# Gated DeltaNet and sliding-window block on one core: GpSimd's weight splits moved behind the first softmax quotient, one sum moved from VectorE to ScalarE

## What is computed

```python
def hybrid_layer(x, norm_w, w_in, conv_w, a_log, dt_bias, gdn_norm_w, attn_sinks,
                 w_o_a, w_o_b, w_out, pos_bias):
    h = rms_norm(x, norm_w)
    z = h @ w_in
    (qa, ka, va, b_a, a_a, za, qb, kb, vb, zb, gate_a, gate_b) = jnp.split(z, SPLIT_POINTS, axis=-1)
    qkv = jax.nn.silu(causal_depthwise_conv(jnp.concatenate([qa, ka, va], axis=-1), conv_w))
...
    qa = l2_normalize(qa.reshape(B, T, GDN_HEADS, GDN_DK))
    ka = l2_normalize(ka.reshape(B, T, GDN_HEADS, GDN_DK))
...
    oa = gated_delta_rule(qa, ka, va, g, beta)
    oa = rms_norm(oa, gdn_norm_w) * jax.nn.silu(za.reshape(B, T, GDN_HEADS, GDN_DV))
    ya = oa.reshape(B, T, GDN_V_W) @ w_o_a
    ob = swa_sink_attention(...)
    ob = ob.reshape(B, T, SWA_Q_W) * jax.nn.silu(zb)
    yb = ob @ w_o_b
    merged = jax.nn.sigmoid(gate_a) * ya + jax.nn.sigmoid(gate_b) * yb
    return x + merged @ w_out
```

## Time and profile before

| | us |
|---|---|
| median of 3 runs | 2635.09 (2634.76 to 2636.34) |
| the profiled execution, its own time | 2636.74 |
| its span in the trace | 2634.9 |
| PE busy | 2594.6 (98%) |
| DVE busy | 1340.2 (51%) |
| ACT busy | 894.6 (34%) |
| POOL busy | 404.8 (15%) |
| SP waits for splits, 60 to 480 us | 355.6 in 48 waits |

### The profile page before, as it was taken

How to read it: one execution, slowest core, us unless ns; L and a number is a source line. 1 busy time by engine, 2 the same in 40 slices (tenths; PEclk the granted TensorE clock), 3 DMA queues, 4 the chain that set the end, 5 groups by cost and what they waited for, 6 DMA issues and landing times.

```text
span 2634.9 us, 50095 instructions
## 1 busy us (share of the span) xinstructions
PE 2594.6 (98%) x20276; PEld 2129.6 (81%) x20276; DVE 1340.2 (51%) x3401; ACT 894.6 (34%) x2886; POOL 404.8 (15%) x238
## 2 busy tenths in 40 slices
PE   7999999999999999999999999999999999999998
PEld 5777777888888888888888888888888888888887
DVE  6577777323266666612325666651223666665022
ACT  4454445332234344321114344432112333434001
POOL 3443334343210011000001011000000011010000
PEclk9999999999999999999999999999999999999999
DMA  7555455687653333355553433335546433333554
GB/s 246 191 205 199 164 185 198 244 282 288 239 182 129 131 135 135 135 192 209 183 215 142 141 131 137 130 125 208 208 176 230 141 119 135 130 131 129 204 211 175
DMA packets 96085, 467.06 MB, mean 177 GB/s; under 512 B 13808, under 2 KB 34544, under 8 KB 48880
## 3 DMA queue, kind: packets, MB, share of 16 engines
q1 hardware_dynamic: 65664, 427.85, 45.1%
q10 hardware_dynamic: 30192, 36.02, 4.6%
HBM read 361.00 MB, written 102.83 MB: 176 GB/s over the span
## 4 chain that ended last, share of the span: by engine, by line
PE 90%; DVE 5%; DMA 1%; POOL 1%; ACT 1%; issue 1%; ACTq 0%; SPq 0%; POOLq 0%; DVEq 0%
PE bank L1321 24%; PE bank L1323 22%; PE bank L1322 22%; PE last_banks L1444 3%; PE last_banks L1432 2%; PE bank L1510 1%; PE bank L1495 1%; PE bank L1424 1%; PE bank L1487 1%; PE bank L1555 1%; PE last_banks L1564 1%; PE bank L1545 1%; PE bank L1540 1%; PE last_banks L1561 1%; PE bank L1502 1%; DMA w_raw<-in_w_tiles 1%
## 5 line engine op out<-in xcount | busy, mean ns | idle before, releaser
L1321 PE MATMUL bank<-hT_hi,w_sl 128*128 128x512 f32 x2112 | 889.6, 421 | 0.0
L1323 PE MATMUL bank<-hT_hi,w_sl 128*128 128x512 f32 x2112 | 826.9, 392 | 0.0
L1322 PE MATMUL bank<-hT_lo,w_sl 128*128 128x512 f32 x2112 | 825.6, 391 | 0.0
L1323 PEld LDWEIGHTS bank<-hT_hi,w_sl 128*128 128x128 f32 x2112 | 396.4, 188 | 86.9
L1321 PEld LDWEIGHTS bank<-hT_hi,w_sl 128*128 128x128 f32 x2112 | 397.6, 188 | 76.7 <-issue 0.9
L1322 PEld LDWEIGHTS bank<-hT_lo,w_sl 128*128 128x128 f32 x2112 | 398.6, 189 | 58.9 <-issue 0.7
L441 POOL TENSOR_TENSOR w_sl<-w_raw,w_sl 128x1024 fp32r<-128x1024 f32 x90 | 218.2, 2428 | 344.4 <-ACT w_sl L525 335.1
L1001 DVE SCALAR_TENSOR_TENSOR area<-zraw,stc,area 128x512 f32<-128x512 f32 x288 | 216.3, 751 | 3.3
L1164 DVE SCALAR_TENSOR_TENSOR s_cur<-s_cur,scs,last_banks 128x128 f32<-128x128 f32 x112 | 38.9, 347 | 189.7 <-PE last_banks L1561 189.7
L460 POOL TENSOR_TENSOR area<-sums_row,sums_at 128x512 f32<-128x512 f32 x32 | 37.1, 1160 | 635.8 <-DVE nmx L1117 594.6
L639 ACT ACTIVATE area<-area 128x512 f32<-128x512 f32 x96 | 60.4, 629 | 215.0 <-DVE area L1001 215.0
(11 more groups left out here) (242 smaller groups left out, 4345.2 us busy)
## 6 DMA issues: line engine op xcount, KB each, us to landing
w_sl<-saved_w SPq DMA_DIRECT2D x270, 1024.0 KB, 4.8
saved_w<-w_sl SPq DMA_DIRECT2D x90, 1024.0 KB, 4.9
w_raw<-in_w_tiles SPq DMA_DIRECT2D x90, 512.0 KB, 5.9
sums_row<-sum_rows ACTq DMA_DIRECT2D x32, 256.0 KB, 6.4
area<-in_x ACTq DMA_DIRECT2D x4, 2048.0 KB, 9.8
area<-in_x ACTq DMA_DIRECT2D x14, 512.0 KB, 7.4
out_y<-area ACTq DMA_DIRECT2D x3, 2048.0 KB, 7.2
bias_sb<-in_bias ACTq DMA_DIRECT2D x32, 128.0 KB, 2.7
```

Of the source, the lines that this page charges most:

```text
L1321: pe.matmul(dst, a_hi, b_hi, start=first, stop=False)
L1322: pe.matmul(dst, a_hi, b_lo, start=False, stop=False)
L1323: return pe.matmul(dst, a_lo, b_hi, start=False, stop=last)
```

## The change

In GpSimd's `head`, `rk` comes first as before; then GpSimd waits for `prob_ready[0]` of this head, does three splits (before: two), the decays, one split (before: two), `rqo`, and two splits. One split fewer stands ahead of the first `rk` (`low(SLOTS - 1)`), one more behind the last head. The sum `ssk` = `ssq` + 4 EPS is now an ACTIVATE of ScalarE behind the keys' squares and ahead of the exponential `dec`; VectorE's instruction for it is gone, in all 32 heads. The wait for `prob_ready[0]` stands in all 32 heads too.

```diff
             def head(h, n1, last):
 
                 power(rk[:, :], ssk[:, :], NT, ssk_ready, n1, rk_ready)
-                low(2)
+                pool.wait_ge(prob_ready[0], n1)
+                low(3)
                 if not last:
                     pool.wait_ge(nmx_ready[1], n1)
                     decays(h + 1, n1 + 1)
-                low(2)
+                low(1)
                 power(rqo[:, :, :].rearrange("p a t -> p (a t)"), qo[:, :, :].rearrange("p a t -> p (a t)"), 2 * NT,
                       qo_ready, n1, rqo_ready)
                 low(2)
...
                 if b == 0:
-                    low(SLOTS)
+                    low(SLOTS - 1)
                 for h in range(H):
                     head(h, b * H + h + 1, h == H - 1)
-                low(GATE_TILES - FILL_GATES - SLOTS - 1)
+                low(GATE_TILES - FILL_GATES - SLOTS)
...
                 squares(ssq[:, 1, :], bch(3), ssq_ready[1], 1, junk_k)
+                act.wait_ge(ssq_ready[1], n1)
+                act.activation(ssk[:, :], ssq[:, 1, :], ACT.Copy, bias=4 * EPS).then_inc(ssk_ready, 1)
                 act.wait_ge(gup_ready, n1)
                 act.activation(dec, exponent[:, :, :], ACT.Exp).then_inc(dec_ready, 1)
                 squares(ssq[:, 0, :], bch(2), ssq_ready[0], 0, junk_q)
-                act.wait_ge(ssq_ready[1], n1)
                 act.wait_ge(ksc_ready, n1)
...
                 dve.tensor_scalar(negc[:, :], sc[:, EGC, :], -1.0, None, ALU.mult)
-                dve.wait_ge(ssq_ready[1], n1)
-                dve.tensor_scalar(ssk[:, :], ssq[:, 1, :], 4 * EPS, None, ALU.add).then_inc(ssk_ready, 1)
                 dve.wait_ge(dec_ready, n1)
```

## The result

The changed kernel took 2658.44 us, the median of 4 runs (2655.33 to 2660.38), beside 2635.59 for the kernel before (2634.76 to 2636.34). The ratio is 1.0084, with a 95% interval of 1.007 to 1.0097. The prediction was 2650.0, range 2640 to 2661, slower: the sign was right and the time lies in the range, but the forecast was 14.5 us more and the medians differ by 22.9. The profiled execution is the fastest of the four (2655.33, span 2653.4), 18.5 us over the span of before. Two single executions in the slow state, 2862.57 us of the kernel of experiment 5 and 8002.8 us of the kernel before, are left out of the ratios.

The account below looks back on a forecast made before the run. TensorE, 98% busy, was bound, its stops at lines 1516 and 1502 caused by GpSimd's splits holding VectorE. Inner heads 11.4, head 0 -0.9, head 7 2.5, gates 1.5: +14.5 on 2635.09, rounded 2650 us, range 2640 to 2661.

Parts of the forecast that it names:

- Part 1: Next head's norms: b0's split behind `rqo` delays a raw load, line 1516 comes 1.4 us later per head (1.0 to 2.0).
- the meeting of `rk` and line 1043: In the norms, VectorE's line 1043 now meets the power `rk` instead of a split: 0.2 us added.
- a strict reading: Port rule: line 1043 would wait for `rk`'s end, 0.5 us more per inner head, 3 us in all, 2653.
- the 1 us at v's transposes: `fo` under b0's split makes v's transposes wait about 1 us for line 1204; taken as absorbed by the stop at line 1516.
- The sign that I gave for it: Expected trace: TensorE's stops at line 1516 grow from 1.4 us to nearly 2 or more.
- Part 2: From line 1516 to 1462: a2's later split delays raw a4 and `yt`, costing 0.5 us per head (0.1 to 0.9).
- The last head: Head 7: 1.4 us for the norms plus 1.1 from line 1516 to 1462, 2.5 later; nothing for its last transposes.
- Part 3: Gate stretch behind the heads: loads 4.8 us later against a slack of 3.3, fifth tile 1.5 us late (0 to 3).
- the sum of all high ends: All terms at their high ends: 6 x 2.9 for inner heads, -0.1 for head 0, 3.5 and 3: 23.8 us.
- The norms win: Rival: contention goes and raw tiles are in time, faster at 2617 us; needs a2's load within 2.1 us; 8%.
- A short second link: Rival: the norms' delay holds, but ScalarE's stop before `yt` is covered; some 5 us in all, 2640; 10%.
- VectorE loses the gap: Rival: a3's split follows a2's at once, so the powers wait for both; 1.5 us in each of 7 heads, 2660; 12%.

Follow-up runs that it names:

- experiment 5: Kernel with each split in a gap of its own, with b0's split moved from ahead of `rqo` to behind it: 2642.59 us, 1.0022 of the kernel before.
- experiment 1: Its three-buffer run: the changed kernel with three buffers for raw tiles instead of two: 2636.29 us, 0.9997 of the kernel before.
- experiment 3: The changed kernel, but in head 7 GpSimd waits for the end of line 1199 before its two splits behind `rqo`: 2657.94 us, 1.008.
- experiments 2 and 4: Only a3 and a4 behind the quotient, other splits as before: 2636.97 us; the same with a2 behind the first powers: 2634.94 us; both with `ssk` on ScalarE.

## Why the prediction was right, and where it fell short

**Part 1** was right in mechanism and somewhat over in size. In head 2 every step has its row: `rqo` ends at 181.20, the split at 183.55, the load of a2 goes out at 183.95 and its high part starts at 189.66, 5.7 later; the squares and `ssk` follow, `rk` ends at 193.07, and TensorE goes on 1.80 later (forecast 1.75). From the end of `rqo` to that of `rk` it is 11.9 us, forecast 12.05, before 10.8. The cost is 1.07 us a head in the mean, near the low end of 1.0. ScalarE's stop for the tile reads 1.3 rather than the 3.7 that I named, because it had stood 6.8 us for the convolution behind the blocked `fo` first; the load's landing is what ended the chain, as said. The value for the meeting of `rk` and line 1043, 0.2, was too much: they overlap in [192.06, 193.07] and [192.54, 193.23] and both have their usual times. The reading behind the 0.2 missed the order: in the kernel before line 1043 began first (187.18, `rk` at 187.34) and `rk` took 1.38, in all eight heads; now `rk` begins first, by 0.48, and takes 1.01. That is also the answer to the rule of the Trainium skill, page "SBUF — State Buffer", section "Who interferes with whom", that whoever issues first has the shared ports for the whole instruction (the section states it for VectorE's two-port modes, the prediction took it over to two SBUF inputs): for the splits the trace agrees, for this power of four elements with line 1043 behind it it does not, and the 3 us that a strict reading would have added are absent.

Calling the 1 us at v's transposes absorbed was right here, since `tt` was late anyway; the three buffers of experiment 1 show that it counts where the load is in time (36.0 us for 34.7). Net Part 1 is a removed cost of 1.4 and an added one of 2.4. The sign that I gave for it was off: the stops at line 1516 did not grow to nearly 2 but stayed at 1.3, since 1.0 of the delay was spent ahead of them at v's. The period was as told, 55.3 us for 55.0.

**Part 2** had the right steps and one wrong term. Head 2: the split starts at +7.22 from line 1516 (forecast +7.3), TensorE gets a2 at +10.07 (forecast +10.1, with the extended split), the load goes out at +10.42 (+10.5). Then it landed in 211.57 - 205.29 = 6.3 us and not in 5.7, so `yt` and line 1462 came at +17.97, not +17.5. I took the minimum of the earlier trace rows, 5.7; this load took 5.8 to 6.6 in the eight heads. Where it took 5.81 and 5.83, in heads 5 and 6, the cost was 0.50 and 0.52, as forecast; at 6.56, in head 4, it was 1.12. Together with what follows for heads 0 and 1, four of the seven heads came out over the high end of 0.9. The store and load of the next tile now follow 2.8 us behind this one (208.07), but they do so in the heads with 5.8 too: what makes the time vary is not shown. Head 1 is 1.2 over head 2, for two things that I had not in view. ScalarE's issue of the `sums_row` load took 1.33 us and not 0.39, ahead of the exponentials, so that the split began at +8.16. And the clock fell: TensorE came to line 1462 only at 157.72, 0.5 after `yt` was there; it is the one head without a wait for ScalarE at that line. Head 0 has the long issue too (1.35): its split began at +7.87, 0.65 later than head 2's, and its load took 6.36, which makes its 1.62. The kernel before had an issue of 1.11 there as well and no loss by it (17.07 us to line 1462, as in the other heads).

```profile
140.83 1.33 ACTq L625 DMA_DIRECT2D sums_row<-sum_rows  x1
```

**The last head** was the step that failed. I used its `rqo`-split pair as a model for the inner heads and did not ask what the *second* split now behind `rqo` does there. In heads 0 to 6 it waits for ScalarE's high part and comes 4.4 us later; in head 7 both tiles were ready, and line 1199 was caught. That is a stop of 2.5 us. And no term of the sum was for the clock, since no stop of the kernel before was followed by a fall: 1.5 more here, and a part of head 1's.

**Part 3** had the right tile and nearly the right size (1.59 in experiment 3, some 0.2 of it that run's own, and 1.2 more at the next tile) and the wrong place in the sum: a stop upstream of the same product covers it.

**How far the time in the range was luck.** The measured difference is 8.4 us over the forecast one: Part 1 gave 2.3 less, Part 2 4.1 more, the gates 1.5 less, the last head's stop and clock, which no term stood for, 4.0 more, and some 4 us have no row. The late loads of Parts 1 and 2 carried the sign, as said; that 2658 lies within the range owes as much to its width as to the sum. In the sum of all high ends head 0 stands with -0.1, where -1.4 and 0.9 make -0.5; that changes nothing.

**The rivals.** "The norms win" needed the load in 2.1 us; it took 5.7. "A short second link" falls with 1.6 us at line 1462. "VectorE loses the gap" falls too: the pair of splits took 5.58 us and not 4.74, because VectorE's convolution line ended first and then the next one got in between. Rows of both engines, head 1:

```profile
146.74 5.55 POOL L441 TENSOR_TENSOR w_sl<-w_raw,w_sl 128x1024 fp32r<-128x1024 f32 x2 [9.95 <-DVE area L1123]
...
147.65 2.43 DVE L1003 SCALAR_TENSOR_TENSOR area<-zraw,stc,area 128x512 f32<-128x512 f32 x1
```

VectorE's line was held under the first split for 1.7 us, no longer. But that alone is dear, as experiments 2 and 4 show in kernels where TensorE waits for no late raw tile (1.9 us a head at line 1444 and its counterpart, 0.4 before); in the changed kernel it was covered by the waits that a2 made anyway.

## What to carry to other kernels

When an engine's work is moved to free another engine, follow what its completion releases: here each moved split also moved a load of 5.7 us or more, and some 18 of the 22.9 us lost were such loads. Follow also what the moved instruction now lies under or over: of the 2.4 us a head that b0's move cost, 1.2 were the load and 1.25 a new contention, with `fo`, against 1.4 of contention removed. Place the interfering instruction by the gaps of the engine that it holds up, one at a time, and not behind one event in a batch: putting b0 back only undid the loss (0.9994), and giving each split its own gap made a gain of 0.5% of it (0.9947). And look at the last iteration on its own: what its queue holds back to back, the inner ones space out.

## What was new about the chip

- VectorE's waiting instruction gets in between two splits that GpSimd has back to back; the second split then starts later (5.55 to 5.59 us for the pair, 4.71 to 4.75 where VectorE had at most a short one waiting).
- The power `rk` with 4 elements a partition (1.01 us) and line 1043 (0.69) run side by side without delay where `rk` begins first, by 0.48 us; where line 1043 begins first, by 0.16, `rk` takes 1.38. A split holds an instruction of 4 elements until its end: `ssk` and `fo` took 2.35 us.
- A stop of TensorE of 2.5 us (2.1 by its matmul rows) was followed by some 3.5 us in which the granted clock was 0.50 and then 0.65, at a cost of some 1.5 us. Stops of 1.6 and 1.9 us by the matmul rows, ahead of line 1462's counterpart in experiment 3, did the same in heads 3 and 0 and not in head 2 (1.88), and a stop of 3.2 us (by the weight loads' rows) at line 1516 in the kernel before had no fall behind it.
- The issue of one DMA on ScalarE's queue, that of `sums_row`, took 1.35 and 1.33 us in the first two heads and 0.39 in the other five, for the same transfer. In experiment 3's trace it took 0.39 or 0.40 throughout, and there the issue just ahead of it, of `bias_sb`, took 1.22 and 1.85 in the first two heads for 0.46 elsewhere.
